# Attention values as fp32 products on two column tiles, the start's rows by products, the last pair's transposes in two parts

## The chip, the cores and the metric

The kernel runs on one core of one Trainium2 chip. The metric is the device time of one execution in microseconds; lower is better. The inputs lie in the chip's memory when it starts, and the host only lays arrays out.

## The reference

A transformer stack for 512 tokens of 1024 features, in fp32. The first block mixes by windowed means (pooling) under a modulation computed from a conditioning row `c`, and then runs a convolved feed-forward net. The second block has forgetting attention, a feed-forward net, a state-space mixer, and another feed-forward net. What matters here is the modulation and the attention:

```python
# modulation: silu(c) @ ada_w + ada_b gives shift, scale and gate, twice
u = modulate(rms_norm(x, mix_pre_g[i]), sh1, sc1)
y = pool_mixer(u, pool_w[j], pool_scale[j])
x = x + g1 * rms_norm(y, mix_post_g[i])

# attention, 16 heads of 64, query blocks of 128
for blk in range(seq_len // Q_BLOCK):
    k_end = q0 + Q_BLOCK
    s = jnp.einsum('bhqd,bhkd->bhqk', qb, kb).astype(jnp.float32) * scale
    s = s + c[:, :, q0:k_end, None] - c[:, :, None, :k_end]
    s = jnp.where(mask, s, -jnp.inf)
    p = jax.nn.softmax(s, axis=-1).astype(vb.dtype)
    outs.append(jnp.einsum('bhqk,bhkd->bhqd', p, vb))
o = o * jax.nn.sigmoid(gate)
return o @ w_out
```

## The kernel before, in words

Each engine has its own instruction list, written out by hand; they meet at semaphores. Features lie on partitions, tokens on columns.

**Precision.** Most products are made of three fp32r passes (`passes`, L1775 to L1778): both operands are split into a high and a low part, and high x high, high x low and low x high are summed. So every operand has a high copy (ACT) and a low part by subtraction (DVE). Some products take fp32 operands directly, in one instruction each of the program: the transposes, the pool mixer (L2015), the broadcasts by ones (`bc`, L1864) and the state-space tables (L2179, L2189, L2194).

**Weights.** They come in slots of 128 x 1024 through a ring of five (`load_fm`, `load_tm` in SP's list); a slot is loaded when the one five before it has been used (`slot_mm`), split by ACT (`hi`, L737) and DVE (`lo`, L1101), and used by TensorE three slots later. In the attention SP also stores a table that POOL makes after every second slot (`turn_store`, L630), waiting for `turn_new_done`.

**Start** (`startup` in each list). SP loads the reciprocal counts, the vectors `vec`, `c` broadcast to 128 partitions, x, the first round of modulation weights `ada` (four buffers; round m is `dot_parts(m)` in DVE's list, 4 x 2 dot products), and the pool weights. TensorE transposes `vec` (L1956), ACT copies it to `vec_t`, SP writes that to a scratch in memory (L570), waits, and reads the row `pool_scale` back, broadcast (L572). TensorE transposes x (L1966), ACT and DVE copy it to `xt`. DVE does rounds 0 to 3, scales the pool weights in between (L1574), then `early_half(0)` (L1117, the first half of the output times the post gain) and `boundary`. ACT, meanwhile, makes diagonals of gains (L752), TensorE turns them into rows on all partitions (`bc`), and ACT copies them to `gpost` and `gpre`. `boundary` (ACT L779, DVE L1147) does, per block of 128 tokens, the norm, the residual, the next norm (`htok`), and in its first block round 4 of the dot products (L1175).

**Attention** (`fox`). First the values of all heads (8 slots) go to `vo_hi` (ACT L959) and `vo_lo` (DVE L1414), one feature block further on than the outputs, which later take the same tiles. Then the forget logits. The loop has eight iterations, one per pair of heads, and one before it. For pair i, with the weights of pair i+1 in between, TensorE does: `scores(i)` (L2032); the q slot of the next pair; six eighths of its k slot, a head sum (L2077) in it; `transposes(i)` (L2042) of the probabilities; the gate slot with the other head sum; `values(i)` (L2059). DVE does `head_out(i-1)` (L1349: gate times values, split in two), `row_max`, `normalize`, `copy_qk` and `make_qk` for the next pair, and the split of the transposes (`pt_split`, L1386). ACT does the exponentials, squares, `attend_pt` (L938: five copies of the transposed probabilities) and the gate. In `values` each head multiplies all 128 columns of the pair's values, in its own PSUM bank, and `head_out` takes the head's half.

```python
for h in range(2):
    for kb in range(QB):
        c, w = PT_AT[kb], T - P * kb
        mm = passes(pv_bank(jj, h)[:, P * kb:T], vo_hi[:, jj + 1, cols], vo_lo[:, jj + 1, cols],
                    pt_hi[:, h, c:c + w], pt_lo[:, h, c:c + w], kb == 0, kb == QB - 1)
```

After the loop `fox_out` (L2153) does the output product: for blocks 0 and 1 of the tokens the first three slots, then the transposes and values of the last pair, then the same slots for blocks 2 and 3, the fourth slot, and `tail` with the boundary.

## Time and profile before

| What | Value |
|---|---|
| median of 3 runs (1747.09 to 1749.04) | 1747.36 us |
| the profiled execution's own time | 1745.99 us |
| its span in the trace | 1744.3 us |
| TensorE products busy | 1656.3 us, 95% |
| TensorE weight loads busy | 1385.6 us, 79% |
| DVE busy | 1008.2 us, 58% |
| ACT busy | 643.4 us, 37% |
| POOL busy | 237.9 us, 14% |
| mean granted TensorE clock | 0.98 |

The shares are averages over stages with different limits, so they say where to look, not what a change is worth. The busy time of a product is from its start to its modelled end, and products overlap; the spacing of starts is what they cost. In the timeline a row is a run of like instructions: start and length in us, engine, line, what is written and read, shape, number, and in brackets the idle time of the engine before it and who ended it. PEld is TensorE's weight load, SPq SP's queue of issues. Products of fp32 operands have two records each (transposes one). The stages by time: start to about 105 us, first feed-forward net to about 490, attention to about 800, then the rest.

### The profile page before, as it was taken

How to read it: one execution, taken by the hardware profiler on the slowest of the kernel's cores; microseconds unless marked ns; L12 is line 12 of the kernel's file. 1: busy time of each engine (PE TensorE's matmuls, PEld its weight loads, DVE VectorE, ACT ScalarE, POOL GpSimd, SP SyncE). 2: the span in 40 equal slices, each digit the busy share in tenths (PEclk: the TensorE clock that was granted, in tenths of full speed). 3: DMA queues.
4: the chain of work that ended last, by engine and by line, in shares of the span. 5: the costliest groups of instructions: out<-in, count | busy, mean ns of one | idle time of the engine just before them, and what ended most of it. 6: DMA issues, size and time to landing. Idle time of an engine off the chain costs nothing.

```text
span 1744.3 us, 21846 instructions
## 1 busy us (share of the span) xinstructions
PE 1656.3 (95%) x8511; PEld 1385.6 (79%) x8511; DVE 1008.2 (58%) x1631; ACT 643.4 (37%) x1033; POOL 237.9 (14%) x745
## 2 busy tenths in 40 slices
PE   4479999999998999999999999999899999999998
PEld 4468888888877888878888888888788888888886
DVE  5888666676655888856333337667636633333223
ACT  4365333323345665745222222333224522222222
POOL 2001700000027766630000000000010000000000
PEclk8779999999999999999999999999999999999999
DMA  8922222345342221223222234467863222223332
GB/s 340 381 81 97 94 95 100 92 128 149 94 116 77 75 67 58 68 91 109 97 97 97 97 97 133 129 187 229 259 158 113 97 97 97 97 97 97 97 97 73
DMA packets 136695, 211.61 MB, mean 121 GB/s; under 512 B 28833, under 2 KB 102929, under 8 KB 133265
## 3 DMA queue, kind: packets, MB, share of 16 engines
q1 hardware_dynamic: 121680, 202.88, 36.4%
q10 hardware_dynamic: 14912, 7.34, 1.6%
q8 instruction: 67, 1.10, 0.3%
q14 instruction: 36, 0.29, 0.1%
HBM read 192.38 MB, written 17.82 MB: 121 GB/s over the span
## 4 chain that ended last, share of the span: by engine, by line
PE 76%; DVE 11%; DMA 6%; issue 3%; ACT 3%; SPq 1%; POOL 0%; ACTq 0%; DVEq 0%; PEldq 0%
PE bank L1776 24%; PE bank L1778 24%; PE bank L1777 24%; DMA raw<-in_dn 1%; DVE prob L1369 1%; DMA ada<-in_ada_w 1%; DVE w_lo L1105 1%; ACT prob L936 1%; DVE ada L1201 1%; DMA gain_scratch<-vec_t 1%; DMA u_scratch<-us 1%; PE bank L1816 1%; PE bank L2189 1%; PE bank L2194 1%; DVE prob L1384 1%
## 5 line engine op out<-in xcount | busy, mean ns | idle before, releaser
L1776 PE MATMUL bank<-hh,w_hi 128*128 128x512 f32 (+1 forms) x1440 | 552.1, 383 | 12.5 <-POOL hl L1771 6.6
L1777 PE MATMUL bank<-hl,w_hi 128*128 128x512 f32 (+1 forms) x1440 | 548.5, 381 | 0.0
L1778 PE MATMUL bank<-hh,w_lo 128*128 128x512 f32 (+1 forms) x1440 | 548.4, 381 | 0.0
L1105 DVE TENSOR_TENSOR w_lo<-raw,w_hi 128x1024 fp32r<-128x1024 f32 x262 | 316.0, 1226 | 191.9 <-ACT w_hi L741 189.7
L741 ACT ACTIVATE w_hi<-raw 128x1024 fp32r<-128x1024 f32 x262 | 275.4, 1056 | 375.5 <-PE bank L1778 119.8
L1776 PEld LDWEIGHTS bank<-hh,w_hi 128*128 128x128 f32 x1440 | 272.1, 189 | 66.7 <-POOL hl L1771 7.1
L1778 PEld LDWEIGHTS bank<-hh,w_lo 128*128 128x128 f32 x1440 | 272.2, 189 | 51.6
L1777 PEld LDWEIGHTS bank<-hl,w_hi 128*128 128x128 f32 x1440 | 272.3, 189 | 50.5
L1776 PE MATMUL bank<-w_hi,hid 128*128 128x512 f32 x528 | 206.9, 392 | 0.7 <-ACT kt L859 0.7
L1778 PE MATMUL bank<-w_hi,hid 128*128 128x512 f32 x528 | 205.6, 389 | 0.0
L1777 PE MATMUL bank<-w_lo,hid 128*128 128x512 f32 x528 | 205.5, 389 | 0.0
L1259 DVE TENSOR_TENSOR scr<-scr,bank 128x512 f32<-128x512 f32 x44 | 30.3, 688 | 289.8 <-PE bank L1778 289.8
L846 ACT ACTIVATE scr<-bank 128x512 f32<-128x512 f32 x44 | 26.3, 598 | 269.3 <-PE bank L1778 269.3
L1776 PEld LDWEIGHTS bank<-w_hi,hid 128*128 128x128 f32 x528 | 99.1, 188 | 23.0 <-issue 1.7
L1778 PEld LDWEIGHTS bank<-w_hi,hid 128*128 128x128 f32 x528 | 99.1, 188 | 20.6
L1777 PEld LDWEIGHTS bank<-w_lo,hid 128*128 128x128 f32 x528 | 99.1, 188 | 20.1
L833 ACT ACTIVATE scr<-bank,convw 128x512 f32<-128x512 f32 x44 | 34.4, 781 | 139.0 <-PE bank L1778 139.0
L1771 POOL TENSOR_TENSOR hl<-yfm,hh 128x512 fp32r<-128x512 f32 x8 | 10.2, 1302 | 529.2 <-ACT hh L1031 529.2
L1234 DVE SCALAR_TENSOR_TENSOR scr<-bank,convw,scr 128x511 f32<-128x511 f32 x44 | 32.9, 749 | 64.2 <-ACT scr L833 64.2
L1627 POOL TENSOR_TENSOR turn_new<-turn_t 128x2 f32<-128x2 f32 (+2 forms) x192 | 64.4, 335 | 15.0
L1201 DVE CUSTOM_DVE_ANT_0 ada<-ada,csil 128x1024 f32<-128x1024 f32 x48 | 56.2, 1221 | 3.0 <-DMA ada<-in_ada_w 2.3
L1627 POOL TENSOR_TENSOR turn_t<-turn_new 128x2 f32<-128x2 f32 (+2 forms) x192 | 55.7, 290 | 0.0
(271 smaller groups left out, 1921.3 us busy)
## 6 DMA issues: line engine op xcount, KB each, us to landing
raw<-in_up SPq DMA_DIRECT2D x132, 512.0 KB, 3.2
raw<-in_dn SPq DMA_DIRECT2D x60, 512.0 KB, 4.1
ada<-in_ada_w SPq DMA_DIRECT2D x24, 1024.0 KB, 7.5
raw<-in_fox_in SPq DMA_DIRECT2D x32, 512.0 KB, 3.4
raw<-in_s_w SPq DMA_DIRECT2D x24, 512.0 KB, 4.2
q_scratch<-q_tab SPq DMA_DIRECT2D x8, 512.0 KB, 4.3
w_scratch<-w_new SPq DMA_DIRECT2D x8, 512.0 KB, 5.1
raw<-in_fox_out SPq DMA_DIRECT2D x8, 512.0 KB, 3.5
```

Of the source, the lines that this page charges most:

```text
L741: act.activation(w_hi[:, n % RING, :], raw[:, n % RING, :], ACT.Copy).then_inc(hi_done, 1)
L833: act.activation(scr[:, 2 * s, :], bank[base + (2 * j + s) % 4][:, :], ACT.Identity, scale=convw[:, j, 4 * s + 1:4 * s + 2], bias=convw[:, ...
L846: act.activation(scr[:, j % 2, :], bank[base + (2 * j) % 4][:, :], ACT.Silu).then_inc(act_done, 1)
L936: act.activation(pr, pr, ACT.Exp, bias=nmax[:, r], accum_out=rsum[:, r]).then_inc(exp_done, 1)
L1105: dve.tensor_tensor(w_lo[:, n % RING, :], raw[:, n % RING, :], w_hi[:, n % RING, :].bitcast(F32), ALU.subtract).then_inc(lo_done, 1)
L1201: dot = dve.tensor_tensor_reduce(wt, wt, csil[:, :], 1.0, 0.0, ALU.mult, ALU.add, accum_out=dots[:, m, 2 * b + t:2 * b + t + 1])
L1234: own.add(dve.scalar_tensor_tensor(c[:, 1:T], b[:, 0:T - 1], convw[:, j, 4 * s:4 * s + 1], c[:, 1:T], ALU.mult, ALU.add))
L1259: dve.tensor_tensor(p, scr[:, j % 2, :], bank[base + (2 * j + 1) % 4][:, :], ALU.mult)\
L1627: own.add(pool.tensor_tensor(out_, a, b, op))
L1776: pe.matmul(dst, w_h, r_h, start=first, stop=False, skip_group_check=True)
L1777: pe.matmul(dst, w_h, r_l, start=False, stop=False, skip_group_check=True)
L1778: return pe.matmul(dst, w_l, r_h, start=False, stop=last, skip_group_check=True)
```

## The change

- **Values.** ACT copies values and transposed probabilities once, in fp32 (`vv`, `pt`); the low parts and DVE's subtractions for them go. Each head multiplies only its own 64 value columns, as one fp32 product per key block, into its own 64 rows of one bank, in the order of `PV_PARTS`, heads in turn, each waiting only for its part of `pt`. `head_out` multiplies by the gate in one instruction.
- **Loop.** The first slot waits for the first half of the values only and no longer for `z_ready`; `scores(0)` waits for all values. The wait for `o_done` stands behind six eighths of the k slot.
- **Last pair.** Its transposes are done in two parts: those of the last query block after the second output slot, the rest after the third. Half of the fourth output slot's products for blocks 0 and 1 stand between transposes and values, half for blocks 2 and 3 behind the other slots.
- **Start.** `c` is loaded as one row and spread by two products with ones; `pool_scale` comes from `vec` by a diagonal (DVE) and eight products with ones, and DVE copies the result. SP waits for the scratch only before it reads gains for the second boundary. `bc(0)` stands behind the first two pool blocks, the early half before the last quarter of round 3, and `gpre`'s diagonal and copies in the first block of the boundary, after its first square and root.

Left out of the diff are the semaphores' declarations.

```diff
+c_row = in_h("c_row", [D], F32, KT * T + D)
+diag_scale = in_hid("diag_scale", [KT, P], F32, 6 * D)
...
-pt_hi = in_hid("pt_hi", [2, NP_], F32R, 2 * NP_)
-pt_lo = in_hid("pt_lo", [2, NP_], F32R, 4 * NP_)
+pt = in_hid("pt", [2, NP_], F32, 2 * NP_)
...
+vv = in_hid("vv", [KT + 1, T], F32, VX)
...
 
-def pv_bank(jj, h):
-    return bank[7] if h == 0 else bank[1 if jj + 1 < KT else 5]
-
-def t_parts(pt):
+PV_BANK = bank[7]
+PV_PARTS = ((0, 0, 0), (1, 0, 1), (0, 1, 2), (1, 1, 3), (0, 3, 2), (1, 3, 3), (0, 2, 4), (1, 2, 4))
+
+def t_parts():
...
         sp.dma_start(rc_row[0:1, e, :, :], dram["rcnt"][:, t0:t0 + EDGE].unsqueeze(0)).then_inc(rcnt_in, 16)
+    sp.dma_start(c_row[0:1, :], dram["c"]).then_inc(c_in, 16)
     sp.dma_start(vec[:, :], dram["vec"]).then_inc(small_in, 16)
-    sp.dma_start(csil[:, :], dram["c"].to_broadcast([P, D])).then_inc(c_in, 16)
...
     sp.dma_start(gain_dram, vec_t[0:ADA_B, :]).then_inc(vec_out, 16)
-    sp.wait_ge(vec_out, 16)
-    sp.dma_start(scale_bc[:, :], gain_row("pool_scale")).then_inc(scale_in, 16)
...
     load_ada(5)
+    sp.wait_ge(vec_out, 16)
...
                 continue
+            if q == 0 and b == 0:
+                act.wait_ge(mod_done, 3)
+                diagonal(diag_amp2, amp2)
+                bc_copy(1, gpre, 4)
...
         own.add(act.activation(scrap[:, :], eps[:, :], ACT.Silu))
+        for h in range(2):
+            act.wait_ge(c_mm, h + 1)
+            act.activation(csil[:, HALF * h:HALF * h + HALF], bank[h][:, :], ACT.Silu).then_inc(csil_done, 1)
         act.wait_ge(vec_mm, 1)
         act.activation(vec_t[0:ADA_B, :], bank[7][0:ADA_B, 0:P], ACT.Copy).then_inc(vec_done, 1)
-        act.wait_ge(c_in, 16)
-        act.activation(csil[:, :], csil[:, :], ACT.Silu).then_inc(csil_done, 1)
...
         bc_copy(0, gpost, 2)
-        act.wait_ge(mod_done, 3)
-        diagonal(diag_amp2, amp2)
-        bc_copy(1, gpre, 4)
...
             act.wait_ge(pv_mm, jj)
-        for t, (src, dst) in enumerate(t_parts(pt_hi)):
+        for t, (src, dst) in enumerate(t_parts()):
             act.wait_ge(pt_mm, 5 * jj + t + 1)
-            act.activation(dst, src, ACT.Copy).then_inc(pth_done, 1)
+            act.activation(dst, src, ACT.Copy).then_inc(pt_done, 1)
...
             src = (bank_b(1, b) if f == 0 else bank_a(1, b))[:, :].rearrange("p (j c) -> p j c", j=4)
-            act.activation(vo_hi[:, 4 * f + 1:4 * f + 5, P * b:P * b + P], src, ACT.Copy).then_inc(vv_hi, 1)
+            act.activation(vv[:, 4 * f + 1:4 * f + 5, P * b:P * b + P], src, ACT.Copy).then_inc(vv_done, 1)
...
             dve.wait_ge(bc_done, 2 if q == 0 else 6)
+        if q == 0:
+            early_bias(q)
...
             dve.tensor_tensor(ya[:, b, :], bank_a(q, b)[:, :], gpost[:, 0:HALF], ALU.mult).then_inc(ya_done, 1)
+        if q:
+            early_bias(q)
+
+    def early_bias(q):
+        dve.wait_ge(sqa_done, TB * (q + 1))
...
         z = gsig[:, jj % 2, :]
-        for h in range(2):
-            r = slice(HD * h, HD * h + HD)
-            own.add(dve.tensor_tensor(z[r, :], pv_bank(jj, h)[r, :], z[r, :], ALU.mult))
+        own.add(dve.tensor_tensor(z, PV_BANK[:, :], z, ALU.mult))
...
 
-    def pt_split(jj):
-        for t, ((src, hi_), (_, lo_)) in enumerate(zip(t_parts(pt_hi), t_parts(pt_lo))):
-            dve.wait_ge(pth_done, 5 * jj + t + 1)
-            dve.tensor_tensor(lo_, src, hi_.bitcast(F32), ALU.subtract).then_inc(pt_done, 1)
-
...
            .then_inc(qk_done, 1)
-
-    def values_low(f):
-        for b in range(TB):
-            dve.wait_ge(vv_hi, TB * f + b + 1)
-            cols = slice(P * b, P * b + P)
-            src = (bank_b(1, b) if f == 0 else bank_a(1, b))[:, :].rearrange("p (j c) -> p j c", j=4)
-            dve.tensor_tensor(vo_lo[:, 4 * f + 1:4 * f + 5, cols], src,
-                              vo_hi[:, 4 * f + 1:4 * f + 5, cols].bitcast(F32), ALU.subtract).then_inc(vv_done, 1)
...
                    .then_inc(wf_split, 1)
-            if idx == 5:
-                values_low(0)
-        values_low(1)
...
                 copy_qk(nxt, 1, n + 1)
-            if i >= 0:
-                pt_split(i)
...
         dve.tensor_copy(rc_edge[:, :, :, :].rearrange("p e g r -> p (e g r)"), bank[6][:, 0:8 * EDGE]).then_inc(rc_done, 1)
+        dve.wait_ge(small_in, 16)
+        dve.wait_ge(ident_done, 1)
+        shape = [P, KT, P]
+        dve.tensor_tensor(diag_scale[:, :, :], ident[:, :].unsqueeze(1).to_broadcast(shape),
+                          vec[:, vcols("pool_scale")].unsqueeze(2).to_broadcast(shape), ALU.mult)\
+           .then_inc(scale_diag, 1)
+        dve.wait_ge(scale_mm, 1)
+        for h in range(2):
+            dve.tensor_copy(scale_bc[:, HALF * h:HALF * h + HALF], bank[5 + 2 * h][:, :]).then_inc(scale_done, 1)
...
             dve.tensor_copy(xt[:, b, HALF:D], bank[2 * b + 1][:, :]).then_inc(xt_dve, 1)
-        dve.wait_ge(csil_done, 1)
+        dve.wait_ge(csil_done, 2)
...
         dve.sem_inc(mod_done, 1)
-        dve.wait_ge(scale_in, 16)
+        dve.wait_ge(scale_done, 2)
...
         dve.sem_inc(mod_done, 1)
-        dot_parts(3)
+        dot_parts(3, (0, 1, 2))
+        early_half(0)
+        dot_parts(3, (3,))
...
         dve.sem_inc(mod_done, 1)
-        early_half(0)
...
         pe.wait_ge(ident_done, 1)
-        pe.wait_ge(small_in, 16)
-        pe.transpose(bank[7][0:ADA_B, 0:P], vec[:, 0:ADA_B], ident[:, :]).then_inc(vec_mm, 1)
...
                   start=True, stop=True).then_inc(rc_mm, 1)
+        pe.wait_ge(c_in, 16)
+        for h in range(2):
+            pe.matmul(bank[h][:, :], ones_f[0:1, :], c_row[0:1, HALF * h:HALF * h + HALF],
+                      start=True, stop=True).then_inc(c_mm, 1)
+        pe.wait_ge(small_in, 16)
+        pe.transpose(bank[7][0:ADA_B, 0:P], vec[:, 0:ADA_B], ident[:, :]).then_inc(vec_mm, 1)
         pe.wait_ge(vec_done, 1)
+        pe.wait_ge(scale_diag, 1)
+        for k in range(KT):
+            mm = pe.matmul(bank[5 + 2 * (k // 4)][:, P * (k % 4):P * (k % 4) + P], ones_f[:, :], diag_scale[:, k, :],
+                           start=True, stop=True)
+        mm.then_inc(scale_mm, 1)
+        pe.wait_ge(csil_done, 2)
...
             pe.wait_ge(x_in[h], 16)
+            if h:
+                pe.wait_ge(scale_done, 2)
...
         pe.wait_ge(corr_done, 4)
-        bc(0, diag_gpost1, 2)
         for b in range(2):
             pool_slot(1, b, bank_b(0, b)[:, :]).then_inc(blk_mm, 1)
+        bc(0, diag_gpost1, 2)
...
 
+    def last_transposes(qbs, done):
+        pe.wait_ge(p_done, 2 * QB * (KT - 1) + done)
+        for part in ([(0, 0)], [(1, 0)], [(0, 1), (0, 3)], [(1, 1), (1, 3)], [(0, 2), (1, 2)]):
+            for h, kb in part:
+                for qb in qbs:
+                    if qb >= kb:
+                        at_ = P_AT[qb] + P * kb
+                        mm = pe.transpose(t_at(h, kb)[:, P * (qb - kb):P * (qb - kb) + P],
+                                          prob[:, h, at_:at_ + P], ident[:, :])
+            if 0 in qbs:
+                mm.then_inc(pt_mm, 1)
+
     def values(jj):
-        pe.wait_ge(pt_done, 5 * (jj + 1))
-        for h in range(2):
-            for kb in range(QB):
-                c, w = PT_AT[kb], T - P * kb
-                cols = slice(P * kb, P * kb + P)
-                mm = passes(pv_bank(jj, h)[:, P * kb:T], vo_hi[:, jj + 1, cols], vo_lo[:, jj + 1, cols],
-                            pt_hi[:, h, c:c + w], pt_lo[:, h, c:c + w], kb == 0, kb == QB - 1)
+        for h, kb, part in PV_PARTS:
+            pe.wait_ge(pt_done, 5 * jj + part + 1)
+            r, c, w = slice(HD * h, HD * h + HD), PT_AT[kb], T - P * kb
+            mm = pe.matmul(PV_BANK[r, P * kb:T], vv[:, jj + 1, P * kb + HD * h:P * kb + HD * h + HD],
+                           pt[:, h, c:c + w], start=kb == 0, stop=kb == 2, skip_group_check=True)
...
 
-    def out_part(idx, blocks, last=False):
+    def out_part(idx, blocks, ks=range(2)):
         n = S_FO + idx
-        for k in range(2):
+        for k in ks:
...
                 pe.wait_ge(sel_done, 3)
+                pe.wait_ge(vv_done, 2 * TB)
...
             else:
-                pe.wait_ge(vv_done, 2 * TB)
-                pe.wait_ge(z_ready, 1)
+                pe.wait_ge(vv_done, TB)
...
                 pe.wait_ge(ln_done, 2 * nxt)
+            fm_part(n + 1, bank[1][:, :], hh, hl, 0, 6)
             if i >= 1:
                 pe.wait_ge(o_done, i)
-            fm_part(n + 1, bank[1][:, :], hh, hl, 0, 6)
...
             out_part(idx, (0, 1))
-        transposes(KT - 1)
+            if idx == 1:
+                last_transposes([QB - 1], 2)
+        last_transposes(range(QB - 1), 2 * QB)
+        pe.wait_ge(lo_done, S_FO + 4)
+        out_part(3, (0, 1), [0])
...
             out_part(idx, (2, 3)).then_inc(slot_mm, 1)
-        pe.wait_ge(lo_done, S_FO + 4)
+        out_part(3, (2, 3), [0])
         pe.wait_ge(o_done, KT)
-        out_part(3, range(TB)).then_inc(slot_mm, 1)
+        out_part(3, range(TB), [1]).then_inc(slot_mm, 1)
```

## Rows read from the trace of the kernel before

**Rows 1.** The page, section 4: shares of the chain by engine.

```profile
PE 76%; DVE 11%; DMA 6%; issue 3%; ACT 3%; SPq 1%; POOL 0%; ACTq 0%; DVEq 0%; PEldq 0%
```

**Rows 2.** Timeline, start: start us, length us, engine, line, operation.

```profile
7.98 0.48 SPq L570 DMA_DIRECT2D gain_scratch<-vec_t  x1
...
25.45 0.34 SPq L572 DMA_DIRECT2D scale_bc<-gain_scratch  x1
```

**Rows 3.** Waits, 0 to 110 us: who for whom, us in all, times, longest.

```profile
DVE yb L1157 <- ACT junk L786: 3.8, 1, 3.8
...
DVE raw L1574 <- DMA scale_bc<-gain_scratch: 3.3, 1, 3.3
...
DVE ada L1201 <- DMA ada<-in_ada_w: 2.3, 3, 1.3
```

**Rows 4.** Timeline, DVE in the start: round 4 of the dot products.

```profile
74.38 1.23 DVE L1201 CUSTOM_DVE_ANT_0 ada<-ada,csil 128x1024 f32<-128x1024 f32 x1 [0.18 <-DVE xt L1164]
...
83.74 1.41 DVE L1185 SCALAR_TENSOR_TENSOR htok<-xt,rn,gpre 128x512 f32<-128x512 f32 x2
```

**Rows 5.** Timeline, start: transposes of x, and ACT's gain rows.

```profile
10.38 5.10 PE L1966 MATMUL bank<-ident,xf 128*128 128x128 f32 x32 [4.88 <-DMA xf<-in_x]
...
65.47 2.45 ACT L754 ACTIVATE diag_amp<-ident,amp 128x128 f32<-128x128 f32 x8 [4.18 <-DVEq L1599]
...
70.22 1.08 ACT L750 ACTIVATE gpre<-bank 128x512 f32<-128x512 f32 x2 [2.30 <-PE bank L1867]
```

**Rows 6.** Timeline, TensorE in one iteration: the values, then the next scores.

```profile
605.54 0.39 PE L1776 MATMUL bank<-pt_hi,vo_hi 128*128 128x512 f32 x1
605.77 0.39 PE L1777 MATMUL bank<-pt_lo,vo_hi 128*128 128x512 f32 x1
...
609.41 0.50 PE L2022 MATMUL bank<-qk 64*128 64x512 f32 x2
```

**Rows 7.** Timeline, fp32 products of pool and states; last, the states' line.

```profile
61.81 5.78 PE L2015 MATMUL bank<-raw,v 128*128 128x256 f32 x26
...
1215.70 1.20 PE L2179 MATMUL bank<-ub,w 128*64 128x64 f32 x32
...
L2179 PEld LDWEIGHTS bank<-ub,w x256: 132/138/138, 1201.8 to 1264.6; 128*64 128x64 f32 x128
```

**Rows 8.** Timeline, TensorE: first scores of iterations 0, 1 and 7.

```profile
556.22 0.50 PE L2022 MATMUL bank<-qk 64*128 64x512 f32 x2 [1.58 <-DVE qk L1406]
...
582.45 0.50 PE L2022 MATMUL bank<-qk 64*128 64x512 f32 x2
...
743.57 0.50 PE L2022 MATMUL bank<-qk 64*128 64x512 f32 x2
```

**Rows 9.** Timeline, iteration 1: the second head sum, and DVE's work.

```profile
600.88 0.50 PE L2079 MATMUL bank<-sq_hi,blk64r 128*128 128x512 f32 x1 [0.39 <-DVE qf L1396]
...
582.56 1.41 DVE L1355 TENSOR_TENSOR gsig<-bank,gsig 64x512 f32<-64x512 f32 x2 [2.45 <-PE bank L1778]
...
600.74 3.07 DVE L1389 TENSOR_TENSOR pt_lo<-bank,pt_hi 128x512 fp32r<-128x512 f32 x5
...
606.36 0.69 DVE L1406 TENSOR_TENSOR qk<-qf,qk 128x512 fp32r<-128x512 f32 x1
```

**Rows 10.** Timeline, TensorE: first slot after the forget logits.

```profile
534.82 0.47 PE L1776 MATMUL bank<-hh,w_hi 128*128 128x512 f32 x1 [0.89 <-issue]
```

**Rows 11.** Timeline, TensorE: last pair's transposes, values, and the output slots.

```profile
755.22 2.40 PE L2048 MATMUL bank<-ident,prob 128*128 128x128 f32 x20 [0.25 <-DVE prob L1384]
760.56 0.59 PE L1776 MATMUL bank<-pt_hi,vo_hi 128*128 128x512 f32 x1 [2.94 <-DVE pt_lo L1389]
...
765.99 0.45 PE L1776 MATMUL bank<-w_hi,vo_hi 128*128 128x512 f32 x1
```

**Rows 12.** Timeline, POOL and SP: one turn table and its store.

```profile
585.34 0.10 POOL L1692 MEMSET turn_new<- 128x2 f32 x1 [2.24 <-DMA turn_scratch<-turn_new]
...
598.69 0.52 SPq L634 DMA_DIRECT2D turn_scratch<-turn_new  x1
```

More of the change, by code:

```diff
@@ L308, in build @@
         mod_done = sem("mod_done")
-        scale_in = sem("scale_in")
+        c_mm = sem("c_mm")
+        scale_diag = sem("scale_diag")
+        scale_mm = sem("scale_mm")
+        scale_done = sem("scale_done")
         vec_out = sem("vec_out")
@@ L378, in build @@
         wf_split = sem("wf_split")
-        vv_hi = sem("vv_hi")
         vv_done = sem("vv_done")
@@ L399, in build @@
         pt_mm = sem("pt_mm")
-        pth_done = sem("pth_done")
         pt_done = sem("pt_done")
```

## The prediction

> **What bounds the kernel.** I read the page first: TensorE carries 76% of the chain that ended last, DVE 11%, DMA 6% [rows 1]. So a microsecond counts where TensorE works or stands. The change touches four stretches, and I read each in the timeline and the waits.
>
> The start, up to about 105 us, is not TensorE's. SP issues the write of the gain scratch at 7.98 and stands on its landing until 25.45 [rows 2], with the second round of modulation weights queued behind it. DVE then waits 3.3 us for the pool scale, 2.3 us in three waits for those weights (the longest 1.3), and 3.8 us for ACT [rows 3]. That last wait is one of order: ACT makes a diagonal (2.45 us from 65.47), TensorE multiplies it, ACT copies the result (to 71.3), and only then comes the square that DVE needs [rows 5]. DVE's chain through the dot products (the fifth round from 74.38 to 83.74 [rows 4]) sets when the first token block is ready.
>
> In the attention loop TensorE is nearly full. Iteration 0 takes 26.23 us (556.22 to 582.45). The six behind it take 161.12 (to 743.57), 26.85 each [rows 8]: 0.62 more, since TensorE waits for DVE's copy in front of the second head sum (0.39 idle, the restart beside it) [rows 9]. Ahead of the loop it stands 0.89 us [rows 10]. Behind it, it waits 2.94 us for the split transposes, and the last values call runs in part at the lower clock, 760.56 to 765.99 [rows 11].
>
> **The change, part by part.**
>
> *A, values.* Before: 24 products per pair, from 605.54 to the next scores at 609.41, 3.87 us [rows 6]. After: 8 fp32 products. An fp32 product is two records; 26 records of 256 columns take 5.78 us, 0.22 each, 0.87 ns a column [rows 7]. A head has 512+384+256+128 = 1280 columns, so 2560 record columns, 2.22 us in its own column tile. Both heads cost that once if the tiles run side by side. The nearest row says they do: the scan's states, also fp32 and 64 columns wide in two column tiles, do 32 records of 64 moving columns in 1.20 us [rows 7]; one after another they would need 32 x 0.056 = 1.8. Two switches of tiling come on top, some 0.2 in all (the first product behind such a switch takes 0.50, not 0.39 [rows 6]). I take 2.4 us, by this row; the ends are 2.2, and 4.44+0.2 = 4.6 one after another. Saved: 1.47 per call, 10.3 us over seven calls (the eighth is in D).
>
> *B, DVE in the loop.* The five subtractions that split the transposes go, and so do the eight that split the values; none is on the path, since TensorE has a weight slot to work on meanwhile. The two 64-row products of head_out (1.41 us for both) become one of 128 rows; such a one reading PSUM takes 0.61 (five in 3.07) [rows 9]. So 0.7 us is saved ahead of the maxima, exponentials, normalisation and the copy that TensorE waits for. That covers the 0.62 barely; I take 0.55 x 6 = 3.3 us, ends 1.5 and 3.7. ACT has as many copies as before. Late next: the second operand's low part, which ends at 607.05 for scores at 609.41 [rows 6, 9]. Its chain hangs on the head sum, so the 2.4 us of slack shrink by A's 1.47 to 0.9, and hold. The wait for o_done moves behind 18 products and was long met.
>
> *C, first slot.* It no longer waits for all values and for the forget logits. The 0.89 idle [rows 10] and the restart go, 1.05 us. The squares and head sums behind start from that slot and shift along; DVE's work on the logits ends before its first square is due. Ends 0 and 1.1.
>
> *D, last pair.* From 755.22 to 765.99 it took 10.77 us [rows 11]. Now eight transposes come one slot earlier and twelve later (20 in 2.40, the same work), six output products (1.4, at the 0.23 from one product of 512 columns to the next [rows 6], taken from behind) cover ACT's first copies, and values costs 2.4 at the full clock. 2.4+1.4+2.4 = 6.2, of which 1.4 was due anyway: 4.8 against 10.77. With the 0.25 idle ahead of the transposes and its restart: 6.4 us, ends 4 and 7. Late next is the last output weight slot: its load is freed by slots that now follow closer, and its slack is near nil; up to 1 us is in the lower end.
>
> *E, start.* (1) The c row is a single row instead of a broadcast ahead of x. TensorE gets two products of 512 columns and eight of 128, by ones, before x's transposes: twice 2048 record columns, 1.8 us each at 0.87, double at the low clock. They begin near 5, where TensorE has nothing; x, which began at 10.38 and took 5.10 [rows 5], begins at 11.4 to 12.9 but at the raised clock (20 transposes in 2.40 [rows 11]), and ends 0.3 earlier to 1.2 later. DVE's new diagonal and two copies fall into its idle time before x. I take 0.2 gained. (2) No wait for the scale: 3.3 [rows 3]. (3) SP issues the second round of weights as DVE frees the buffers, not after 25.45: two of the three waits go, 1.0; the third (1.3) stays, since SP's small issues in front of that round follow DVE's own pace. (4) Early half, bias and ACT's square now come before the last quarter of the fourth round: the 3.8 [rows 3] goes. Diagonal, broadcast and copies, 5.8 in all (65.47 to 71.3 [rows 5]), now lie beside the fifth round, 9.4 long [rows 4]; without that cover they would cost up to 5.8. The post-gain broadcast moves behind two pool blocks and is ready about 1 us before the early half. Sum 0.2+3.3+1.0+3.8 = 8.3; ends 4 and 12 (the third wait gone too, and the clock up one step sooner under the first weight slots).
>
> **Sum.** 10.3+3.3+1.05+6.4+8.3 = 29.4. Against the profiled execution's own time, 1745.99: 1716.6. The median of the three runs is 1.37 above it, so 1718.0; I give **1718**. A difference of 0.2%, 3.5 us, is about what a measurement of this kernel can tell from none.
>
> **Rivals.**
>
> *Tiles in turn.* The two column tiles take turns, so the change does not do what its words say. For it: the states row has 64 moving columns, not 512. Against: that row itself. Values cost 4.6: 8 x 2.2 = 17.6 less is gained, 11.8 in all, **1736**.
>
> *Weight loads exposed, slower.* If no weight load ran beside a product in the values call, its 16 records would stand with 16 loads of 0.138 [rows 7]: 4.44+2.2+0.2 = 6.85 us. Of the 29.4, 17.6 are left without A's 8 x 1.47; 8 x (6.85-3.87) = 23.8 are lost: 6.2 slower, **1753**. It decides from 6.1 us a call. Against it: the states block would last 32 x 0.194 = 6.2 us, not 1.20 [rows 7]. The Trainium skill (TensorE: Matmul & The Clock Gate, "Part 3: Packing small matmuls — row/col tiling") states that a weight load overlaps running products only where the row groups differ; two column tiles of full height share all rows, and by that rule this rival would come true. The trace of the states disagrees, so I give it little.
>
> *Pool tables set the pace.* Every second load in SP's queue is followed by a store that waits for POOL's turn tables, and the ring loads stand behind it. One table with the landing of the store before it took 2.24 and 13.35, 15.6 us (up to 598.69) [rows 12]; 1.5 of them an iteration are 23.4, and my iteration is 26.85-0.55-1.47 = 24.8. The margin is 1.4. If they took 18 each, 27 an iteration, the weights would come late and the loop's gain would go, 13.6 less: **1732**.
>
> *The start pays half.* Another wait takes the fourth one's place (the post gain, or the weights late): 4.2 less, **1722**.
>
> **How the numbers follow.** Forecast 0.57, start pays half 0.14, pool tables 0.12, in turn 0.12, loads exposed 0.03, no change for a reason I do not see 0.02. The upper bounds of A to E together add 0.1 to 1.6 each and 3.7 for E, and the profile's 1.4 may lie either way: 1718 less 7 or 8, **1710**. The upper end takes in the pool pace, **1732**. Left out are the tiles in turn and the rest, 0.19. Faster by over 0.2%: 0.95; within: 0.02; slower: 0.03.
>
> **What would show it.** Values: records in pairs, 2.4 us from the first to the next scores. Iterations of 24.8 without idle at the second head sum. No idle before the first slot; no 2.94 behind the last transposes and no fall of the clock near there (where a 512-column product now shows 0.59 instead of 0.39 [rows 11, 6]). SP free of the scratch write; no DVE wait for scale or ACT; the fifth round at about 66. Wrong if values last over 4 us, if SP's store waits turn into ACT's waits for weights, or if DVE waits anew in the start.

## The result, and the profile after

The changed kernel takes **1719.04 us**, median of 4 runs (1717.39 to 1720.48), against 1747.7 us (1747.09 to 1749.04, 4 runs): ratio 0.9835, 95% interval 0.9818 to 0.9852. It was forecast at 1718. The profiled execution took 1719.88 us, its span is 1718.1.

The page of the changed kernel, its head and sections 1 and 4:

```profile
span 1718.1 us, 21714 instructions
...
PE 1652.8 (96%) x8467; PEld 1369.4 (80%) x8467; DVE 974.6 (57%) x1578; ACT 642.7 (37%) x1034; POOL 238.4 (14%) x745
...
PE 90%; DVE 4%; DMA 4%; issue 1%; ACT 1%; POOL 0%; ACTq 0%; SPq 0%; DVEq 0%; PEldq 0%
```

TensorE carries 90% of the chain that ended last, where it carried 76% [rows 1]. Most of the 14 points are stretches in which it waited for DVE, for ACT or for the landing of a load (20% of the chain before, 9% now).

A good way to say where time went is the lag: the start of a TensorE product in the trace of before, less the start of the same product (same names, same count) in the trace after. It changes only where the kernels differ in speed. The gain of a stretch is the lag at its end less the lag at its start.

| stretch, us in the trace of before | forecast | gained |
|---|---|---|
| start, to 150 | 8.3 | 8.47 |
| first slot, to the first scores at 556 | 1.05 | 1.04 |
| loop, 556 to 744 | 10.3 + 3.3 = 13.6 | 13.55 |
| last pair and what follows, 744 to 800 | 6.4 | 5.58 |
| 800 to 1150 | 0 | 0.00 |
| scan, 1150 to the end | 0 | -2.47 |
| sum | 29.4 | 26.17 |

**Start.** Timeline of the changed kernel:

```profile
14.41 2.48 DVE L1558 COPY xt<-bank 128x512 f32<-128x512 f32 x4 [0.90 <-PE bank L1979]
...
26.83 2.36 DVE L1574 TENSOR_TENSOR raw<-raw,scale_bc 128x1024 f32<-128x1024 f32 x2 [0.21 <-DVE amp L1223]
...
50.64 1.22 DVE L1212 CUSTOM_DVE_ANT_0 ada<-ada,csil 128x1024 f32<-128x1024 f32 x1 [1.06 <-DMA ada<-in_ada_w]
...
63.45 0.69 DVE L1168 TENSOR_TENSOR yb<-bank,gpost 128x512 f32<-128x512 f32 x1 [0.21 <-DVE amp L1223]
...
65.84 1.23 DVE L1212 CUSTOM_DVE_ANT_0 ada<-ada,csil 128x1024 f32<-128x1024 f32 x1 [0.18 <-DVE xt L1175]
```

The 3.3 us for the scale, the 3.8 for ACT and two of the three waits for weights [rows 3] are gone; the third stays (1.06). The fifth round begins at 65.84 instead of 74.38 [rows 4]. Only x's copies came later, 14.41 against 14.21.

**Loop.** Timeline, TensorE: first scores of iterations 0, 1 and 7, and the values call ahead of the last of them. The waits of TensorE from 556 to 748 us have no row at all.

```profile
546.71 0.50 PE L2035 MATMUL bank<-qk 64*128 64x512 f32 x2
...
571.52 0.50 PE L2035 MATMUL bank<-qk 64*128 64x512 f32 x2
...
718.20 2.37 PE L2088 MATMUL bank<-pt,vv 128*64 128x512 f32 x16
...
720.50 0.50 PE L2035 MATMUL bank<-qk 64*128 64x512 f32 x2
```

Values to scores is 2.30 us (3.87 before [rows 6]); the six later iterations take 148.98, 24.83 each (26.85 before [rows 8]), and the 0.39 at the second head sum [rows 9] is gone.

**Last pair.** Timeline, TensorE, the same kernel; then ACT's splits of the last output weights.

```profile
728.80 1.03 PE L2079 MATMUL bank<-ident,prob 128*128 128x128 f32 x8
...
732.42 1.47 PE L2079 MATMUL bank<-ident,prob 128*128 128x128 f32 x12
...
735.22 2.37 PE L2088 MATMUL bank<-pt,vv 128*64 128x512 f32 x16
...
750.56 1.06 ACT L743 ACTIVATE w_hi<-raw 128x1024 fp32r<-128x1024 f32 x1 [5.13 <-DMA raw<-in_fox_out]
752.24 1.06 ACT L743 ACTIVATE w_hi<-raw 128x1024 fp32r<-128x1024 f32 x1 [0.62 <-DMA raw<-in_fox_out]
...
752.93 0.50 PE L1777 MATMUL bank<-w_hi,vo_hi 128*128 128x512 f32 x1
...
754.62 0.50 PE L1777 MATMUL bank<-w_hi,vo_hi 128*128 128x512 f32 x1
```

There is no wait of 2.94 and no lower clock [rows 11]. But the weights of the last two output slots land late: their first products come 0.50 and 0.42 us behind their neighbours instead of 0.23 (the length of 0.50 marks a restart), and 1.12 of the 6.70 us gained by then are given back by 800: 0.7 at these two slots, 0.4 where TensorE takes up the first normalised block of the boundary.

**Scan.** Waits of TensorE between 1110 and 1300 us, the changed kernel, then the kernel before (us in all, times, longest):

```profile
PE bank L2206 <- DMA ub<-u_scratch: 5.2, 4, 2.3
PE bank L1777 <- POOL hl L1772: 3.9, 2, 2.3
```

```profile
PE bank L1776 <- POOL hl L1771: 6.6, 2, 4.9
PE bank L2179 <- DMA ub<-u_scratch: 1.1, 2, 0.9
```

TensorE waits 4.1 us longer for the scratch and 2.7 less for POOL; all its waits in the stretch come to 12.0 us, 10.7 before. And the granted clock is half (1.2 for 2.4 GHz) for 10.2 us here (from 1226.95), for 6.8 in the trace of before (from 1255.76). The change touches nothing here, so the question is whether the loss belongs to it.

### The profile page after: what moved, and what is told of

The parts are those of the page before. It is cut to its first block, busy times and chain, and to the rows that moved or that the text cites. A ratio compares the mean times of both kernels' runs of the same rounds, so it can differ in the third digit from the quotient of the medians.

```text
span 1718.1 us, 21714 instructions
## 1 busy us (share of the span) xinstructions
PE 1652.8 (96%) x8467; PEld 1369.4 (80%) x8467; DVE 974.6 (57%) x1578; ACT 642.7 (37%) x1034; POOL 238.4 (14%) x745
## 4 chain that ended last, share of the span: by engine, by line
PE 90%; DVE 4%; DMA 4%; issue 1%; ACT 1%; POOL 0%; ACTq 0%; SPq 0%; DVEq 0%; PEldq 0%
PE bank L1777 27%; PE bank L1778 27%; PE bank L1779 27%; DVE ada L1212 2%; DMA u_scratch<-us 1%; PE bank L2088 1%; PE bank L1817 1%; PE bank L2061 1%; PE bank L1908 1%; PE bank L2216 1%; PE bank L2221 1%; DMA raw<-in_fox_in 1%; DMA ada<-in_ada_w 1%; DMA ub<-u_scratch 0%; DMA raw<-in_fox_out 0%
## 5 line engine op out<-in xcount | busy, mean ns | idle before, releaser
L1772 POOL TENSOR_TENSOR hl<-yfm,hh 128x512 fp32r<-128x512 f32 x8 | 10.2, 1298 | 523.9 <-ACT hh L1035 523.9
```

## The experiments

All times are medians; the kernel before, beside them, gave 1748.76, 1749.52, 1749.31 and 1748.48 us. Runs of one kernel scatter by 1 to 7 us, so for terms under 3 us the lag at a place is the measure, and the whole time only agrees or not.

**Order of the two heads.**

```
-PV_PARTS = ((0, 0, 0), (1, 0, 1), (0, 1, 2), (1, 1, 3), (0, 3, 2), (1, 3, 3), (0, 2, 4), (1, 2, 4))
+PV_PARTS = ((0, 0, 0), (0, 1, 2), (0, 3, 2), (0, 2, 4), (1, 0, 1), (1, 1, 3), (1, 3, 3), (1, 2, 4))
```

> The changed kernel, with the eight fp32 products of each values call in another order: the four of head 0, then the four of head 1, instead of one of each in turn. All else equal. If the two column tiles gain because products of different tiles that follow each other run side by side, the neighbours are now in the same tile and the call takes about 16 records of 0.22 to 0.11 us by width, 4.4 us instead of 2.3: 8 x 2.1 = 17 us more, about 1736. If a product of 64 columns simply runs at twice the rate, whoever its neighbour is, the call stays at 2.3 and the time at 1719. If weight loads inside one tile are not hidden, each of 16 records also stands for 0.06 to 0.14 us: 5.4 to 6.7 us a call, 1744 to 1754.

1733.19 us (1732.72 to 1735.86), ratio 0.9912 (0.9898 to 0.9927). The call takes 3.86 instead of 2.30 us:

```profile
728.10 3.93 PE L2088 MATMUL bank<-pt,vv 128*64 128x512 f32 x16
731.96 0.50 PE L2035 MATMUL bank<-qk 64*128 64x512 f32 x2
```

So neighbours matter, and a narrow product is not simply fast. In the changed kernel the records of the two heads start in pairs, 7 ns apart. Here head 0's first records start alone, at 0, 0.48, 0.91, 1.23 and 1.55 us, and head 1's first one 6 ns behind the fifth, ahead of three of head 0's that come before it in the program. So TensorE takes a record of the other tile a little early, and no earlier than that. That is why it is 3.86 and not the 4.4 that I expected. (The expectation's "0.22 to 0.11 us by width" is a slip: a record of 512 columns takes 0.43, and its sum of 4.4 goes by that.) Between records of one tile there is 0.43 us for 512 columns, 0.84 ns a column, the same as at full width (next run); the 16 weight loads of a call, 0.13 to 0.14 us each, add nothing.

**No column tiles.** Each head's products take all 128 weight columns and a bank of their own:

```
-                    mm = pe.matmul(PV_BANK[r, P * kb:T], vv[:, jj + 1, P * kb + HD * h:P * kb + HD * h + HD],
+                    mm = pe.matmul(pv_bank(jj, h)[:, P * kb:T], vv[:, jj + 1, P * kb:P * kb + P],
                                    pt[:, h, c:c + w], start=kb == 0, stop=kb == 2, skip_group_check=True)
```

(with head_out's product in two halves, the wait for `o_done` ahead of the slot, and all parts of `pt` awaited before the first product)

> The changed kernel with fp32 values but without column tiles: each head's product takes the weights of both heads (128 columns) and writes a bank of its own, head_out takes its two halves in two operations, and the wait for o_done stands ahead of the slot again, since that bank is used there. If the tiles do the work of two side by side, a call takes 16 records one after another, 4.4 to 4.6 us: 8 x 2.2 = 17.6, and 0.45 x 6 = 2.7 for the longer head_out, about 1739 (a single-pass fp32r call took 3.87, so this is slower than the three-pass form of before). If column tiling adds nothing to fp32, calls stay near 2.3 and the time within 1719 to 1722.

1738.01 us (1737.74 to 1738.78), ratio 0.9938 (0.9923 to 0.9952), within 1 us of the expectation. A call takes 4.41 us:

```profile
732.61 4.48 PE L2094 MATMUL bank<-pt,vv 128*128 128x512 f32 x16
737.02 0.50 PE L2041 MATMUL bank<-qk 64*128 64x512 f32 x2
```

That is more than the 3.87 of three fp32r passes (which the expectation calls single-pass by mistake): fp32 alone would have been a loss of 0.54 a call, and the column tiles are what turns it into a gain of 1.57. The longer head_out brings the stall back as well (TensorE's waits, 556 to 748 us):

```profile
PE bank L2108 <- DVE qf L1406: 1.7, 6, 0.4
```

**head_out in two halves.**

```
-    own.add(dve.tensor_tensor(z, PV_BANK[:, :], z, ALU.mult))
+    for h in range(2):
+        r = slice(HD * h, HD * h + HD)
+        own.add(dve.tensor_tensor(z[r, :], PV_BANK[r, :], z[r, :], ALU.mult))
```

> The changed kernel with only head_out's product in two operations of 64 rows again. If the single operation is what took TensorE's stall at the second head sum away, 0.7 us comes back on DVE ahead of that copy and TensorE loses about 0.45 in each of six iterations: 2.7, about 1721.7, with idle time in front of the second head sum again. If the removed low-part subtractions took the stall away, nothing comes back: 1719, and no idle there.

1723.16 us (1722.28 to 1726.71), ratio 0.985 (0.9834 to 0.9867). The wait is back in each of six iterations:

```profile
PE bank L2104 <- DVE qf L1402: 1.4, 6, 0.3
```

The loop's gain falls from 13.55 to 10.71: 2.84 us, 0.47 an iteration. An iteration takes 25.30, and 26.85 of before less 1.57 for the values is 25.28: with two operations in head_out nothing but the values is gained, though the subtractions are gone. One DVE operation instead of two (0.69 us for 1.41) took TensorE's stall away; the removed subtractions did not.

**Last pair in the order of before.**

```
-                    if idx == 1:
-                        last_transposes([QB - 1], 2)
-                last_transposes(range(QB - 1), 2 * QB)
-                pe.wait_ge(lo_done, S_FO + 4)
-                out_part(3, (0, 1), [0])
+                transposes(KT - 1)
                 values(KT - 1)
```

(and the fourth slot whole, behind the second halves of the first three)

> The changed kernel with the last pair in the order of before: all twenty transposes behind three half slots, values right behind them, the fourth slot whole at the end. ACT's five copies are 0.5 us each and begin 0.6 after the first transpose, so the last lands about 3.2 us after the transposes began, and the products take its parts in that order. If most of the 6.4 us came from fp32 values (no low part to wait for, no fall of the clock), this order costs only the wait for the weights' normalised rows and up to 0.5 behind the transposes: 0.3 to 1.0 more, 1719.3 to 1720, and TensorE's clock stays up. If the order itself was what took the wait away, 3 us and the lower clock come back: 1722 to 1724.

1719.74 us (1718.35 to 1721.52), as far as whole times can tell the same. Timeline, TensorE:

```profile
733.07 2.35 PE L2061 MATMUL bank<-ident,prob 128*128 128x128 f32 x20
735.34 2.37 PE L2088 MATMUL bank<-pt,vv 128*64 128x512 f32 x16
```

Values follow the twenty transposes without a wait. The gain is 6.79 us when the pair is done, against 6.70 with the new order, so the new order hides nothing: fp32 values did it, since no low part has to be made. And 6.77 are left at 800, where the new order keeps 5.58 (5.60 when that kernel was profiled again). The six products of the fourth slot that it puts ahead of values delay the second halves of slots 0 to 2, those free the ring, and the last weights are asked for 1.4 us later relative to the work. The expectation looked for a loss of 0.3 to 1.0; it is a gain of 1.2. Other traces bear this out: the eight profiles with the new order and the gains' loads in their place, the slowed tables aside, lose 0.8 to 1.1 between 770 and 800, the two with the old order and fp32 values nothing. But the start alone, with the old order and the old values, loses 0.8 there too, so the old order has no slack to spare either.

**Attention alone, start alone.** The two parts of the change, each on the kernel before.

> The kernel before with only the edits from the values slots to the output product (fp32 values in column tiles, first slot's waits, head_out in one operation, last pair's order); the start is as before. By the two traces' difference these stretches gave 13.5 (loop), 1.05 (first slot) and 6.4 less 1.1 (last pair): 19.9 us, about 1727.8. If the stretches are not additive (the clock or the weights' loads differ by when the stretch begins), it differs from that by more than 1.5.

> The kernel before with only the edits of the start (c row and pool scale by products, early half inside the fourth round, post gain behind two pool blocks). First weight slot at about 91.8 instead of 100.3 us: 8.5 us, about 1739.2.

1730.69 (1729.32 to 1731.7) and 1741.09 (1738.46 to 1741.2): 18.8 and 8.4 less than the kernel before beside them. The loop gives 13.52 and the pair 6.70, less 0.82, much as in the whole change; the first slot gives 1.1 here and nothing in the kernel with the start alone. The first time is 2.9 above its expectation. Of these, 1.8 are the kernel before, which gave 1749.52 beside it and 1747.7 in the result that the expectation starts from; the 1.1 left are within the scatter. Its trace is slow in two places that are not the edits': its first weight slot, behind a start that is line for line the old one, comes at 102.21 us where the trace of before has 100.33, and its scan loses 2.26.

**Early half late again.**

```
-                dot_parts(3, (0, 1, 2))
-                early_half(0)
-                dot_parts(3, (3,))
+                dot_parts(3)
...
+                early_half(0)
                 boundary(0, S_UP1)
```

(with ACT's second diagonal and copies ahead of its square)

> The changed kernel with the early half behind the fourth round again, and ACT's second diagonal and its copies ahead of the square, as before. If the order was worth what I took, DVE waits again for ACT's square behind diagonal, product and copies, about 3.8 us, and the fifth round begins near 69.6: 1722.8. If the wait merely moves (the fifth round hides it elsewhere), less than 1: 1719 to 1720.

1726.58 us (1722.17 to 1727.65). The profiled execution is the fastest of the four; the others took 1725.76 and more. The wait for ACT is back, and the fifth round begins 5.0 us later than in the changed kernel, 0.6 of which is there at x's copies already (15.03 for 14.41):

```profile
68.47 0.69 DVE L1167 TENSOR_TENSOR yb<-bank,gpost 128x512 f32<-128x512 f32 x1 [3.91 <-ACT junk L788]
...
70.87 1.23 DVE L1211 CUSTOM_DVE_ANT_0 ada<-ada,csil 128x1024 f32<-128x1024 f32 x1 [0.18 <-DVE xt L1174]
```

**Pool scale through DRAM again.** The diagonal, eight products and two copies are left out; SP waits for the gain scratch and loads the scale from it.

> The changed kernel with the pool scale through the gain scratch in DRAM again (SP waits for the write's landing, then loads it in broadcast), the products and copies for it left out; the c row stays a product. 3.3 us of wait for the scale and about 1.0 of waits for the second round's weights return, less up to 0.5 in x's transposes: first slot 3.8 to 4.3 later, about 1723. If the weights' waits were not the scratch's doing, 3.3: 1722.3.

1719.85 us (1719.49 to 1721.29). Less than expected, and the trace tells why:

```profile
13.03 2.48 DVE L1551 COPY xt<-bank 128x512 f32<-128x512 f32 x4 [8.61 <-PE bank L1965]
...
27.88 2.36 DVE L1567 TENSOR_TENSOR raw<-raw,scale_bc 128x1024 f32<-128x1024 f32 x2 [2.64 <-DMA scale_bc<-gain_scratch]
33.88 1.23 DVE L1212 CUSTOM_DVE_ANT_0 ada<-ada,csil 128x1024 f32<-128x1024 f32 x1 [1.12 <-DMA ada<-in_ada_w]
```

The waits of 2.64 and 1.12 come back, but x's copies begin at 13.03: the scale's products had stood in front of x's transposes and cost 1.4 us in the profiled execution (x's copies at 14.28 to 15.61 in the nine others that have them there). The fifth round begins at 68.29, 2.45 later, so making the scale on TensorE was worth 2.45 and not 3.8 to 4.3. At 150 us 1.74 of it is left, and the whole times show no difference.

**Slower turn tables.** One fill and eight products of 0.41 us more in each table, 3.5 us by the trace:

```
+                own.add(pool.memset(turn_t[:, 1, :, :], 1.0))
+                own.settle()
+                for _ in range(8):
+                    tt(turn_t[:, 0, :, :], turn_t[:, 1, :, :], turn_t[:, 1, :, :], ALU.mult)
```

> The changed kernel with one fill and eight more products of 128 x 124 to 128 on GpSimd in each turn table, about 0.3 to 0.4 us each: 2.5 to 3.5 us more a table. Tables with their stores took 15.6 us; 1.5 of them stand against an iteration of 24.8. If GpSimd's pace decides from 16.5 us a table, 18.5 makes an iteration 27.8 against 24.8 once the ring's lead is used up: 10 to 20 us slower, 1729 to 1739, with ACT waiting for weights in the loop. If SP's stores cost the loads nothing, 1719.

1769.33 us (1768.94 to 1770.26), 50 more than the changed kernel. SP's waits from 560 to 720 us, here and then in the changed kernel:

```profile
SPq L636 <- POOLq L1715: 145.6, 8, 20.1
SPq L519 <- PE bank L1783: 0.7, 1, 0.7
```

```profile
SPq L519 <- PE bank L1779: 74.8, 13, 10.3
SPq L636 <- POOLq L1711: 44.9, 10, 7.6
```

Slowed, GpSimd alone sets SP's pace, a store every 19.7 us (581.03 to 699.29 for six), and the six later iterations take 30.1. Less the 3.5, a table takes 16.2 us, 24.3 for the one and a half of an iteration: by this estimate the changed kernel's 24.83 stand 0.5 us above the next limit. From the iterations themselves it is less: 30.08 less one and a half times 3.5 is 24.83, nothing to spare. The size was off since I let the lead of the ring absorb much; between 535 and 800 us of the trace of before it loses 47 us against the changed kernel, 13 or 14 tables at 3.5.

**Gains behind the last weights, and the changed kernel again.** SP issues the two gain loads behind the last output weights and waits for the first one:

```
                     sp.dma_start(gpost[:, :], gain_row(POST[q])).then_inc(gain_in, 16)
+                    if q == 2:
+                        sp.wait_ge(gain_in, 32)
...
-                if idx == RING:
+                if idx == KT - 1:
```

> The changed kernel with the two broadcast loads of the gains issued behind the last output weights instead of between the fifth and the sixth to eighth (and SP waiting for the first of them). In the changed kernel the seventh took 7.2 us to land and TensorE began the last two output slots 0.7 us late. If the gains' loads were what delayed it, the last two slots start without idle time: 0.7 us less, 1718.3. If the ring itself is the limit, the same; if the gains then land late for the half tiles behind, up to 1 slower.

> The changed kernel once more, as the measure for the one beside it: 1719, and in the scan's stretch another draw of the waits for the scratch's return and of the clock; if the 2.5 us that this stretch lost against the kernel before is chance, its loss differs from that by over 1 us here; if it belongs to the change, it is 2.5 again.

1720.25 (1718.17 to 1721.38) and 1719.64 us (1718.22 to 1722.12). With the gains behind them the last two slots start without a gap, so the gains' 1 MB had been in front of those weights (the seventh lands in 3.9 us instead of 7.2). But now the next stage's first weights are late: SP issues them at 753.70, behind its wait for the first gain (landed at 753.29), and they land at 758.4. ACT, DVE's low part and with it DVE's norm of the first block wait for them, and TensorE for the block. The gain `gpre` itself, landed at 757.1, is not what they wait for. ACT, DVE and TensorE:

```profile
758.43 1.06 ACT L745 ACTIVATE w_hi<-raw 128x1024 fp32r<-128x1024 f32 x1 [2.98 <-DMA raw<-in_up]
759.52 1.23 DVE L1111 TENSOR_TENSOR w_lo<-raw,w_hi 128x1024 fp32r<-128x1024 f32 x1 [2.65 <-ACT w_hi L745]
...
765.54 0.66 PE L1819 MATMUL bank<-ident,htok 128*128 128x128 f32 x4 [1.31 <-DVE htok L1198]
```

It keeps 4.88 at 800 where the changed kernel keeps 5.58: a loss of 0.7, within the expectation's "up to 1 slower".

The second profile of the changed kernel loses 1.23 us in the scan, the first 2.47. Over all kernels, whose code there is the same, the loss against the one profile of before is 0.2, 0.4, 0.5, 0.6, 1.2, 1.4, 1.8, 2.3, 2.5, 2.9, 3.1 and 4.8 us, and the last kernel below gains 1.1. The clock goes with it: it is half for 6.8 us of the scan in the trace of before and in the five that lose 0.6 or less or gain, for 10.2 to 13.7 us in the eight that lose 1.2 and more. The scan's time differs from execution to execution by when the scratch comes back and how long the clock is low, and the trace of before was one of the lucky ones. Nothing shows a part of it that belongs to the change: the medians of before and after are 28.7 us apart in the result and 29.7 here, and the lags ahead of the scan alone make 28.6 and 29.0.

**The two corrections together.** The old order of the last pair, and the scale's products behind x's transposes with their copies on ACT:

```
                 mm.then_inc(rs_mm, 1)
+                pe.wait_ge(scale_diag, 1)
+                for k in range(KT):
+                    mm = pe.matmul(bank[5 + 2 * (k // 4)][:, P * (k % 4):P * (k % 4) + P], ones_f[:, :],
+                                   diag_scale[:, k, :], start=True, stop=True)
+                mm.then_inc(scale_mm, 1)
                 pe.wait_ge(rs_done, 1)
+                pe.wait_ge(scale_done, 2)
```

> The changed kernel with two edits: the last pair in the order of before (as in the run of that name), and the eight products for the pool scale behind x's transposes and the edge sums, their two copies on ACT instead of DVE. First: in the changed kernel x's copies began on DVE at 14.28 to 15.6 us, in the run without these products at 13.03; if they are what delays x, the copies begin near 13.0 here, DVE finds no wait for the scale (it asks for it about 11.5 us later), and the first weight slot comes 1.3 to 2.5 us earlier than the changed kernel's 91.8; if x's own load is the limit, nothing changes there. Second: the last two output slots start without idle time, 1.1 less at the point 35 us behind. Together 2.4 to 3.5 less: 1716 to 1717; less if the modulation weights' loads, not DVE, then set the pace.

1717.88 us (1714.91 to 1718.76, 5 runs), ratio 0.9821 (0.9807 to 0.9834); the changed kernel run again had 0.9833 (0.9818 to 0.9848), so the whole times do not tell them apart. In the trace both edits do what they were made for. x's copies, the scale's use without a wait for it, and the first weight slot (91.80 in the changed kernel, 91.71 when it was profiled again):

```profile
13.18 2.48 DVE L1558 COPY xt<-bank 128x512 f32<-128x512 f32 x4 [7.23 <-PE bank L1972]
25.60 2.36 DVE L1574 TENSOR_TENSOR raw<-raw,scale_bc 128x1024 f32<-128x1024 f32 x2 [0.21 <-DVE amp L1226]
...
90.34 0.55 PE L1777 MATMUL bank<-hh,w_hi 128*128 128x256 f32 x1 [1.61 <-DVE w_lo L1112]
```

And the last pair keeps 6.77 at 800. That is 1.4 and 1.2 us; a fall of the clock at 474 us took 1.8 back (last section). The whole time is above the 1716 to 1717 that I expected.

## Why the prediction held, and where it did not

The forecast case came true and the time, 1719.04, is 1.0 us from it. That is luck in part. Against the profiled executions the sum was 3.3 us too good (1716.6 for 1719.88): 2.5 in the scan, 0.8 in the last pair. The execution profiled before lay 1.4 us under the median that I had and the one after 0.8 over its own, and these two took most of the miss out again.

*A.* Right, by its own row: the states' 1.20 us block carried over to products of 512 columns. 1.57 a call and 11.0 in seven calls, against 1.47 and 10.3; of the 0.2 for two switches 0.1 was there. The rival in which the tiles take turns is real when the order lets it be: one head after the other costs 1.56 us a call.

*B.* Right in mechanism, and in size within its bounds: 13.55 less 11.0 leaves 2.6 for 3.3, 0.45 an iteration for 0.55, and putting the two halves back cost 0.47.

*C.* Right: the first slot follows the forget logits at their own pace (525.33 behind 525.10, no idle), and 1.04 came of 1.05. No run undoes this edit alone; the two halves of the change show it, about 1.1 with it and nothing without.

*D.* The size up to the values held, 6.70 for 6.4, but the reason did not. The step that failed is "six output products cover ACT's first copies": nothing was there to cover, as the old order with fp32 values waits for nothing and gains 6.79. What the prediction named as late next, the last output slots' weights, came true at 1.1 us, just over the "up to 1", and it is the new order that made them late.

*E.* The sum held, 8.47 for 8.3, by errors that cancel. (1) I took 0.2 gained ahead of x; it was 0.2 lost in this execution (14.41 for 14.21), inside the bounds of 0.3 earlier to 1.2 later, and 1.4 in the latest of the others. It has two parts: without the scale's products, but with the c row, x's copies begin at 13.03, so the row gained 1.2 against the trace of before and the products cost 1.4. (2) and (3) The scale and two of the weights' waits went as said, 3.85 for 4.3; with the 1.4 that the products cost, making the scale on TensorE was worth 2.45. (4) The 3.8 for ACT was real, and more came with it: 5.0 when it is undone, 4.4 without what x's copies were late by. What makes up the rest was not looked for.

*The other rivals.* Weight loads exposed: shown false. With products of one column tile in a row, 512 columns still take 0.43 us, the same as at full width, and a call of the changed kernel takes 2.30 us, not 6.85. The Trainium skill (TensorE: Matmul & The Clock Gate, "Part 3: Packing small matmuls — row/col tiling") says that a load overlaps only products in other row groups; all these products use every row, and neither the changed kernel nor the run with the heads in turn shows a load's time, so for this kernel the measurement decides against the rule as the page states it. Pool tables: the mechanism is real and did not act, with at most 0.5 us an iteration to spare where I had counted 1.4. Start pays half: false. The chances of what is left out of the range add up to 0.17, not 0.19.

*What I left out* is that the one profile of before is itself one execution among several that differ. The old start reached its first slot at 100.33 us in one profile and 102.21 in another, the new one, unaltered, at 91.7 to 92.8.

## What to carry to other kernels

fp32 instead of three fp32r passes pays where two narrow products can be paired in column tiles, and only if they are issued by turns: 2.30 us paired, 3.86 one head after the other, 4.41 untiled, 3.87 as split passes. Before reordering work to cover a wait, ask whether the wait survives the rest of the change, and what the moved work pushes back: here it delayed the release of the ring and cost 1.2 us. And when work is put on an engine that idles early in a kernel, look at what stands in its queue behind it (x's transposes, 1.4 us).

## What the runs showed of the hardware

- **Two column tiles run side by side only when their products alternate, or nearly.** With four products (eight records) of head 0 in front, head 1's first record starts beside the fifth and its second only 0.05 us behind head 0's last. How TensorE chooses is not shown.
- **A wait of about the same length lowers the clock in one execution and not in the next.** At the same products (474.82 us in the changed kernel, 483.25 before) TensorE waits for the same weights in every kernel. In the changed kernel and in the run with the last pair's old order, timeline, TensorE:

```profile
474.82 0.47 PE L1777 MATMUL bank<-w_hi,hh 128*128 128x512 f32 x1 [1.57 <-DVE w_lo L1109]
475.12 0.40 PE L1778 MATMUL bank<-w_lo,hh 128*128 128x512 f32 x1
```

```profile
474.92 0.77 PE L1777 MATMUL bank<-w_hi,hh 128*128 128x512 f32 x1 [1.88 <-DVE w_lo L1109]
475.48 0.63 PE L1778 MATMUL bank<-w_lo,hh 128*128 128x512 f32 x1
```

  In the second the granted clock is half for 3.41 us from 474.65, and 1.7 us are lost for 0.3 more of waiting. It fell so in seven of the fourteen profiles, behind waits of 1.43 to 1.88 us, and not in the others, behind 1.45 to 1.90. One such fall is more than the last pair's order is worth, and one reason why whole times could not rank these variants.
- **A fall can cost nothing.** In the changed kernel the clock is half again from 540.87 to 544.29, behind a wait of 1.96 us for the first head sum (in the trace of before it stays up behind 1.99). The lag falls from 9.57 to 8.02 and is back at 9.51 by the first scores: ahead of these TensorE waited 1.58 us for DVE anyway [rows 8].
- **When the clock rises decides how late x comes.** The 32 transposes of x, in the changed kernel and in the kernel with the start alone, timeline, TensorE:

```profile
12.02 3.66 PE L1979 MATMUL bank<-ident,xf 128*128 128x128 f32 x32
```

```profile
12.14 4.70 PE L2001 MATMUL bank<-ident,xf 128*128 128x128 f32 x32
```

  In the first they start 0.11 us apart from the beginning; in the second the first ten are 0.21 apart, and only from 14.27 on it is 0.11: the higher clock is granted at 11.81 in one and at 14.26 in the other, though TensorE had done the same work before (the scale's products, from 8.63 and 8.56). Over the nine profiles with this start the rise lies between 11.55 and 14.37, x's copies begin at 14.28 to 15.61, and the first weight slot, but for the early half's own 5 us, at 91.7 to 92.8. Why it rises earlier in one execution than in another is not shown.
